# A layer norm boundary between two projections: operand units built in pairs, and one normalisation moved ahead of one low-half split

## What is computed

```
    y = jnp.einsum("bse,ed->bsd", y, w_out) + b_out
    return layer_norm(DEEPNORM_ALPHA * x + y, ln_g, ln_b)
...
    h = rms_norm(x, g_mix)
    (q, k_c, v_c, k_s, v_s, k_w, v_w, g_logit,
     q_l, k_l, v_l, a_l, r_l) = jnp.split(h @ w_in, split_points(), axis=-1)
```

## Time and profile before

| | us |
|---|---|
| median of 3 runs | 1756.42 |
| lowest and highest run | 1750.64 and 1760.66 |
| the profiled execution, its own time | 1753.29 |
| the span of its profile | 1751.2 |

### The profile page before, as it was taken

The page is one execution under the profiler, slowest core; times in us unless marked ns, Lnnn a source line. Parts: engine busy times, 40 slices in busy tenths (PEclk is TensorE's granted clock), DMA queues, the critical chain, the costliest instruction groups (busy, mean ns, idle before and its releaser), DMA issues.

```text
span 1751.2 us, 21788 instructions
## 1 busy us (share of the span) xinstructions
PE 1661.3 (95%) x7929; PEld 1369.0 (78%) x7929; DVE 1076.7 (61%) x1531; ACT 776.5 (44%) x1025; POOL 16.7 (1%) x46
## 2 busy tenths in 40 slices
PE   7999898997899999899998999999999999999998
PEld 6877676786667887787887788888878888888787
DVE  5699996667655666977566555445545445544453
ACT  4433455433433455334554464444433344444332
POOL 3000000000000000000000000000000000000000
PEclk9999999999998999999999999999999999999999
DMA  7574342463375453335554355555555555555553
GB/s 262 200 252 154 118 165 78 168 201 130 127 240 183 130 177 108 111 101 219 185 172 157 127 168 193 192 189 186 184 184 192 192 192 193 192 192 190 172 193 117
DMA packets 160285, 301.40 MB, mean 172 GB/s; under 512 B 5508, under 2 KB 24738, under 8 KB 159697
## 3 DMA queue, kind: packets, MB, share of 16 engines
q1 hardware_dynamic: 159520, 300.14, 51.3%
q0 software_dynamic: 688, 0.23, 0.1%
HBM read 298.26 MB, written 2.10 MB: 172 GB/s over the span
## 4 chain that ended last, share of the span: by engine, by line
PE 81%; DVE 11%; issue 3%; ACT 2%; DMA 1%; DVEq 0%; SPq 0%; ACTq 0%
PE ps_g L347 25%; PE ps_g L349 24%; PE ps_g L348 24%; DVE cT L1750 3%; DVE lo L366 3%; PE ps_m L279 2%; DMA raw<-in_w_in_dram 1%; ACT hi L358 1%; PE ps_m L1055 0%; PE ps_m L997 0%; PE ps_m L840 0%; PE ps_m L939 0%; PE ps_m L920 0%; DVE x L1915 0%; PE ps_m L1005 0%
## 5 line engine op out<-in xcount | busy, mean ns | idle before, releaser
L366 DVE TENSOR_TENSOR lo<-raw,hi 128x1024 fp32r<-128x1024 f32 (+3 forms) x552 | 653.3, 1186 | 543.4 <-ACT hi L358 534.9
L358 ACT CAST hi<-raw 128x1024 fp32r<-128x1024 f32 (+3 forms) x552 | 562.2, 1021 | 783.1 <-PE ps_g L349 758.7
L347 PE MATMUL ps_g<-hi,aH 128*128 128x512 f32 (+3 forms) x1696 | 668.9, 394 | 14.9 <-DVE lo L366 9.9
L348 PE MATMUL ps_g<-lo,aH 128*128 128x512 f32 (+3 forms) x1696 | 653.3, 385 | 0.0
L349 PE MATMUL ps_g<-hi,aL 128*128 128x512 f32 (+3 forms) x1696 | 653.3, 385 | 0.0
L347 PEld LDWEIGHTS ps_g<-hi,aH 128*128 128x128 f32 x1696 | 325.6, 192 | 81.8 <-issue 21.5
L349 PEld LDWEIGHTS ps_g<-hi,aL 128*128 128x128 f32 x1696 | 324.6, 191 | 63.9
L348 PEld LDWEIGHTS ps_g<-lo,aH 128*128 128x128 f32 x1696 | 325.9, 192 | 59.2 <-issue 0.5
L347 PE MATMUL ps_g<-hi,guH 128*128 128x512 f32 x352 | 137.1, 390 | 0.0
L349 PE MATMUL ps_g<-hi,guL 128*128 128x512 f32 x352 | 137.0, 389 | 0.0
L348 PE MATMUL ps_g<-lo,guH 128*128 128x512 f32 x352 | 136.9, 389 | 0.0
(11 more groups left out here) (365 smaller groups left out, 1112.7 us busy)
## 6 DMA issues: line engine op xcount, KB each, us to landing
raw<-in_w_gu_dram SPq DMA_DIRECT2D x88, 1024.0 KB, 5.0
raw<-in_w_in_dram SPq DMA_DIRECT2D x76, 1024.0 KB, 6.1
raw<-in_w_down_dram SPq DMA_DIRECT2D x44, 1024.0 KB, 5.0
raw<-in_w_out_dram SPq DMA_DIRECT2D x32, 1024.0 KB, 5.2
raw<-in_w_ck_dram SPq DMA_DIRECT2D x8, 1024.0 KB, 5.5
raw<-in_w_cv_dram SPq DMA_DIRECT2D x8, 1024.0 KB, 6.6
raw<-in_w_in_dram SPq DMA_DIRECT2D x12, 512.0 KB, 3.6
raw<-in_w_cq_dram SPq DMA_DIRECT2D x4, 1024.0 KB, 5.3
```

Source lines behind the costliest of these rows:

```text
L347: pe.matmul(dst, xh, wh, start=first, stop=False)
L348: pe.matmul(dst, xh, wl, start=False, stop=False)
L358: act.copy(step_view(hi, s), raw_view(s)).then_inc(s_hi, 1)
L366: dve.tensor_tensor(step_view(lo, s), raw_view(s), step_view(hi, s).bitcast(F32), ALU.subtract).then_inc(s_lo, 1)
```

## The change

`h_T` and `h_hi` are called with two units at j = 0, 2 and 4, where they were called with one unit at j = 0 to 5. On DVE the normalisation of quarter 4 comes right after L4 and L5, ahead of S5; S5 follows it, and S6 stands after L6 and L7.

```diff
@@ PE
-                    if g["name"] == "ncmp" and j < 6:
-                        h_T([j + 2])
+                    if g["name"] == "ncmp" and j in (0, 2, 4):
+                        h_T([j + 2, j + 3])
@@ ACT
-                    if g["name"] == "ncmp" and j < 6:
-                        h_hi([j + 2])
+                    if g["name"] == "ncmp" and j in (0, 2, 4):
+                        h_hi([j + 2, j + 3])
@@ DVE
             layer_norm_rows(2 * NG, 3 * NG)
             keep_up(first + 1)
             h_lo([4, 5])
+            layer_norm_rows(3 * NG, D)
             keep_up(first + 2)
-            layer_norm_rows(3 * NG, D)
-            keep_up(first + 3)
             h_lo([6, 7])
             keep_up(first + 6)
```

## The result

| | us |
|---|---|
| the changed kernel, median of 5 runs (lowest to highest) | 1740.94 (1737.17 to 1745.10) |
| the kernel before, median of 5 runs | 1755.38 (1750.64 to 1760.66) |
| ratio, with its 95% interval | 0.9914 [0.9889, 0.9939] |
| profiled execution, its own time, after and before | 1737.17 and 1753.29 |

What follows compares the result with a forecast made beforehand. PE waits on quarters from DVE, which waits on units that wait for PE; DVE's work plus idle time bounds the stretch. 8.6 us to the `pc` transposes plus 1.7 of clock gives 10.3: 1746.1 us, range 1741.5 to 1751.5.

Steps and rivals of the forecast that it cites:

- The loop PE, unit, DVE: Between T2 and the `pc` transposes: PE waits for a quarter, DVE is late from awaiting a unit, the unit awaited PE.
- The sum to the transposes behind `pc`, 8.6: From T2 on, the same durations placed in the new order bring the transposes behind `pc` 8.6 us earlier.
- What is late next: Moving S5 and S6 opens two short PE waits, 0.2 us ahead of G5 and 0.7 ahead of G6.
- POOL: POOL's constants move beside S5 to S7: cost nothing; as rival, DVE loses 2.5 us, gain 7.8, 1748.6 us, chance 0.05.
- The clock behind `pc`, 1.7: Lower clock from 471.0 to 474.6, behind the `pc` transposes, goes as their stall shrinks: 1.7 us, bounds 0 and 1.7.
- The clock falls anyway: Rival: the clock still drops behind the `pc` transposes, so the gain is 8.6 us, 1747.8 us; chance 0.17.
- Little: Rival: the lists don't interlock as thought, T3 or T5 awaiting a bank, say; gain 3 us, 1753.4 us; chance 0.07.
- slower: Rival: S5 becomes late and holds up G5 and all PE behind it; 1762 us if 16 late; chance 0.02.
- Given back: Rival: in the next groups transfers set the pace and PE waits longer; half lost, 5 us, 1751.3 us; chance 0.11.

Runs made afterwards that it cites:

- the three waits filled: Kernel before, with unread matmuls put into PE's waits ahead of T4 (8), T6 (12) and the transposes behind `pc` (8): 1754.32 us against 1755.96, ratio 0.9985.

## Why the prediction was right, and where it wasn't

- **The loop PE, unit, DVE.** Right. L3 stands directly behind L2, L5 behind L4, and T4 and T6 have no wait. Pairs alone gave 7.7 of 8.6.
- **The sum to the transposes behind `pc`, 8.6.** Measured 8.61 between the two first profiles (47.43 and 38.82 from T0). T4 and T6 came 6.39 and 12.72 behind T2, forecast 6.33 and 12.65. The fourth profile of the kernel before had 47.40; the second and third had 48.94 and 50.25, with more falls of the clock on the way. Without any fall it is 7.0 (45.84 with the three waits filled).
- **What is late next.** Right in place and nearly in size: G6 waits 0.59 (0.7), G5 about 0.1 (0.2). That G6's wait costs nothing by itself was only shown by the run with S6 between L6 and L7; G5's was in that run too and is untested.
- **POOL.** The cover holds: S6 to S8 took 3.58 together where three took 3.42 without POOL beside them, 0.16 of DVE.
- **The clock behind `pc`, 1.7.** Right for the execution it was read from: from the transposes behind `pc` to the first product 11.72 before and 10.19 after, 1.53, and 10.14 in all against 10.3. That this came out so near is in part luck: the execution that it was read from had two falls in this part, others three and five.
- **The failed step is the clock as a term of one execution.** I counted two stretches at the lower clock between T2 and the first product (one in the 8.6, one as the 1.7), took the waits as things that either lower the clock or don't, and named T4's 1.96 as one that doesn't. And I put any difference of the clock behind the first product at nothing: the waits there were to follow unchanged, and I took equal waits to get an equal clock. Neither held. Of six executions with a wait of 1.93 to 1.96 ahead of T4, the clock fell at T4 in three, 0.8 behind its start in a fourth, and not in two. Four profiles of the kernel before had 2, 3, 5 and 2 stretches between T2 and the first product. On their mean that part takes 53.0 us, in the changed kernel 41.5: 11.5, of which 6.9 is waiting and 4.6 clock, not 3.3. Behind the first product the same code had 5 to 11 stretches at about 1.65 us, and in the two profiles compared first it was 9 against 5: 6.9 us that the forecast had at 0.
- **What put the time outside the range.** The second of the two. The first five runs of the changed kernel had a mean clock of 0.986, all 23 one of 0.9845, and their medians are 1740.9 and 1743.9. The part behind the first product alone differs by up to 10.5 us between executions of the same code, and medians of five move with it. With 11.5 in place of 10.3 the forecast from the median of the 68 runs is 1744.2, near the 1743.9; but the two repeated measurements, 10.1 and 8.6 by medians and 9.9 by means, lie as near to 10.3, so the times can't tell the 11.5 from it.
- **The range.** Below it allowed a gain of 11.5 and a base 3.1 lower, and nothing for the changed kernel's own runs. The sum also has a slip: 1753.3 - 11.5 is 1741.8, not 1741.5. The bounds 0 and 1.7 for the clock were drawn around one reading.
- **Waits and clock in the runs.** At a granted clock of 0.984 (rounded), 12 runs of the changed kernel and 14 of before have means of 1744.5 and 1751.5, 7.0 apart, as the waiting alone would give; at 0.982, 4 and 16 runs, it is 5.9. Over all runs the means are 11.2 apart and the mean clocks 0.9845 and 0.9824; at 1.65 to 2 us for each 0.001 the clock makes 3.4 to 4.2 of that.
- **The rivals.** *The clock falls anyway*: it was at 1.00 up to the first product in all three profiles of the changed kernel. *POOL*: 0.16 us of DVE. *Little* and *slower*: no, by the rows above. *Given back*: not in time at an equal number of stretches, where both kernels follow one line; whether the changed kernel has as many stretches there stays open, since the profiles had 5, 9 and 5 against 9, 11, 5 and 7, and too few to tell.

## What to carry to other kernels

Where one engine builds operands for another in single units, and a later piece of its input hangs behind them in a queue, look whether the unit waits for the very engine that it feeds; issuing two units together can break the loop at no cost, and moving the later piece alone may only move the wait. A stretch at the full clock repeats closely (41.51, 41.50 and 41.53 us here), the granted clock behind waits doesn't: take the clock from several profiled executions, and split a gain into waits and clock before judging a difference of half a per cent.

## What the runs showed of the hardware

A wait of PE of 1.93 to 1.96 us ahead of T4 was followed by a stretch at the lower clock (1.2 GHz) in four of six executions and by the full 2.4 GHz in two, and one of 3.1 us ahead of T6 by one stretch or two. Ahead of the head transposes one of 3.27 us was followed by none in one execution, one of 2.70 by one in another. I had taken this as fixed by the length of the wait.

In the changed kernel it was mostly POOL that paid where it met DVE, beside S6 to S8:

```profile
445.76 1.28 POOL L699 TENSOR_SCALAR_AFFINE_SELECT visc<-visc 128x2 f32<-128x2 f32 x1
```

The same instruction took 0.19 us in the kernel before, where no weights' half ran beside it; the last of POOL's list (L703) took 0.91 and 0.29. S8, on DVE, took 1.31 where the others took 1.22. In the third profile of the changed kernel L699 began 0.06 ahead of S6, not 0.02, and took 0.19. Both read SBUF, as the weights' low halves do with both inputs. The Trainium skill ("SBUF — State Buffer", two separate sides) says that such a pair exclude each other; this trace agrees, as far as POOL's 1.1 us goes.
